# Expert weights loaded as one whole expert per block instead of half of two experts

## The reference

```
hg  = einsum('td,edf->tef', t, w_gate)     # 16 experts, 1024 -> 512
hu  = einsum('td,edf->tef', t, w_up)
act = silu(hg) * hu * combine              # two experts of one group per token
out = einsum('tef,efd->td', act, w_down)   # 512 -> 1024
```

## Time and profile before

| what | value |
| --- | --- |
| median of 3 runs | 2135.21 us (2132.83 to 2135.38) |
| the profiled execution's own time | 2134.79 us |
| its span, first to last instruction | 2133.0 us |
| TensorE matmul busy | 1902.6 us, 89% |
| TensorE weight load busy | 979.1 us, 46% |
| VectorE / ScalarE busy | 445.3 / 375.9 us |
| bytes moved by DMA | 597.12 MB, mean 280 GB/s |
| packets of SP's queue | 105840 of 583.29 MB |
| mean granted clock of TensorE | 0.935 of full speed |

### The profile page before, as it was taken

One profiled execution on the slowest core, in us unless ns is written; L12 is line 12 of the kernel. 1 busy time (PEld: TensorE's weight loads), 2 busy tenths in 40 slices (PEclk: granted clock), 3 DMA queues, 4 the chain that ended last, 5 costly groups with the idle time before them and its releaser, 6 DMA issues.

```text
span 2133.0 us, 19763 instructions
## 1 busy us (share of the span) xinstructions
PE 1902.6 (89%) x8458; PEld 979.1 (46%) x8458; DVE 445.3 (21%) x992; ACT 375.9 (18%) x674; POOL 67.2 (3%) x86
## 2 busy tenths in 40 slices
PE   3987899989998999989988899998999997899996
PEld 1552334436555334436544534335885654443432
DVE  0120011120053011120012201112345582201112
ACT  1120101111042101121010211002223341211111
POOL 1000000000000000000000000000002420000000
PEclk7988999999978999999999799999999999899998
DMA  9458999995842799985872299996341231379994
GB/s 341 190 225 354 421 418 420 421 368 212 342 176 79 320 411 421 420 339 197 316 276 79 79 413 421 419 421 258 120 161 55 80 104 49 119 291 420 416 422 205
DMA packets 109597, 597.12 MB, mean 280 GB/s; under 512 B 6208, under 2 KB 6304, under 8 KB 47936
## 3 DMA queue, kind: packets, MB, share of 16 engines
q1 hardware_dynamic: 105840, 583.29, 68.2%
q0 software_dynamic: 3664, 12.49, 1.8%
HBM read 591.56 MB, written 4.19 MB: 279 GB/s over the span
## 4 chain that ended last, share of the span: by engine, by line
PE 70%; DMA 20%; DVE 5%; ACT 4%; issue 1%; SPq 0%; POOL 0%; DVEq 0%; ACTq 0%; POOLq 0%
DMA ring<-in_moe_w_down 15%; PE psum L454 15%; PE psum L900 13%; PE psum L447 11%; PE psum L882 6%; PE psum L929 5%; PE psum L950 5%; DMA ring<-in_ada_w 4%; PE psum L480 3%; PE psum L513 2%; PE psum L851 1%; PE psum L795 1%; PE psum L778 1%; PE psum L779 1%; ACT arena L1271 1%
## 5 line engine op out<-in xcount | busy, mean ns | idle before, releaser
L900 PE MATMUL psum<-ring,arena 128*64 128x512 f32 x2048 | 449.6, 596 | 10.0 <-DMA ring<-in_moe_w_up 5.2
L900 PEld LDWEIGHTS psum<-ring,arena 128*64 128x64 f32 x2048 | 144.1, 137 | 300.7 <-issue 283.1
L929 PE MATMUL psum<-ring,arena 128*64 128x512 f32 x1024 | 234.5, 600 | 39.3 <-DMA ring<-in_moe_w_down 35.1
L447 PE MATMUL psum<-at,ring 128*128 128x256 f32 x1024 | 229.7, 387 | 4.5 <-ACT at L1075 4.5
L447 PEld LDWEIGHTS psum<-at,ring 128*128 128x128 f32 x1024 | 198.1, 194 | 38.5 <-ACT at L1075 5.6
L454 PE MATMUL psum<-ring,arena 128*128 128x512 f32 x384 | 169.9, 605 | 8.1 <-DVE arena L1533 5.7
L1673 DVE TENSOR_TENSOR arena<-arena,psum 128x512 f32<-128x512 f32 x32 | 33.7, 1053 | 656.8 <-PE psum L900 656.8
L929 PEld LDWEIGHTS psum<-ring,arena 128*64 128x64 f32 x1024 | 71.6, 137 | 195.6 <-issue 133.7
L454 PE MATMUL psum<-ring,at 128*128 128x512 f32 (+1 forms) x352 | 144.6, 565 | 0.0
L480 PE MATMUL psum<-ring,condT 128*32 128x512 f32 x768 | 104.8, 687 | 37.9 <-DMA ring<-in_ada_w 33.7
L882 PE MATMUL psum<-arena,xn 128*128 128x256 f32 x512 | 123.4, 403 | 8.7 <-DVE arena L1459 8.7
(11 more groups left out here) (240 smaller groups left out, 1400.0 us busy)
## 6 DMA issues: line engine op xcount, KB each, us to landing
ring<-in_moe_w_gate SPq DMA_DIRECT2D x64, 2048.0 KB, 13.8
ring<-in_moe_w_up SPq DMA_DIRECT2D x64, 2048.0 KB, 16.1
ring<-in_moe_w_down SPq DMA_DIRECT2D x64, 2048.0 KB, 10.8
ring<-in_ada_w SPq DMA_DIRECT2D x48, 2048.0 KB, 12.6
ring<-in_ssd_w_in SPq DMA_DIRECT2D x12, 2048.0 KB, 8.5
ring<-in_gmlp_w_in SPq DMA_DIRECT2D x8, 2048.0 KB, 11.4
ring<-in_na_w_qkv SPq DMA_DIRECT2D x6, 2048.0 KB, 15.5
ring<-in_gmlp_w_out SPq DMA_DIRECT2D x4, 2048.0 KB, 11.4
```

Of the source, the lines that this page charges most:

```text
L447: last = nc.tensor.matmul(dst, slot(k)[:, c, m * P:(m + 1) * P], src[:, c, :], start=(c == 0), stop=(c == nk - 1))
L900: last = nc.tensor.matmul(ps[b][e * CAP:(e + 1) * CAP, :], rows, slot_pair(k, 4)[:, e, c, :], start=(h == 0 and c == 0), stop=(h == 1 and ...
L929: last = nc.tensor.matmul(ps[6 + j][e * CAP:(e + 1) * CAP, :], actT[:, 2 * h + c, e * CAP:(e + 1) * CAP], slot_pair(k, 2)[:, e, c, j * SLO ...
```

## The change

An expert block now holds **all rows of one expert**: `G{x}.0` is the gate matrix of expert 2x and `G{x}.1` that of expert 2x + 1, and likewise for up and down. A partition's part of one block is then one contiguous run of 16 KB of the matrix instead of two runs of 8 KB. The number of blocks, their size, their order and the ring stay as they are.

Since the two experts of a pair are multiplied in alternation, row group by row group, a product now waits for both of its blocks before its first matmul, and frees both slots after its last one. The matmuls, their operands' shapes and their order are the same. The core of the diff:

```diff
-        def slot_pair(k, c):
+        def slot_expert(k, c):
-            return ring[:, k % RING, :].rearrange("p (e c n) -> p e c n", e=2, c=c)
+            return ring[:, k % RING, :].rearrange("p (c n) -> p c n", c=c)
...
-                    x, h = (int(v) for v in w[1:].split("."))
-                    c = 2 if w[0] == "D" else 4
+                    x, e = (int(v) for v in w[1:].split("."))
+                    c = FF // P if w[0] == "D" else DC
...
-                    load(k, slot_pair(k, c), rows[:, 2 * x:2 * x + 2, c * h:c * h + c, :])
+                    load(k, slot_expert(k, c), rows[:, 2 * x + e, :, :])
...
                 def pair_rows(x, w, b):
-                    for h in range(2):
-                        k = AT[n, f"{w}{x}.{h}"]
-                        arrive(k)
-                        for c in range(4):
-                            for e in range(2):
-                                rows = xg[:, x // 2 % 2, 4 * h + c, (x % 2) * P + e * CAP:(x % 2) * P + (e + 1) * CAP]
-                                last = nc.tensor.matmul(ps[b][e * CAP:(e + 1) * CAP, :], rows, slot_pair(k, 4)[:, e, c, :],
-                                                        start=(h == 0 and c == 0), stop=(h == 1 and c == 3))
-                        last.then_inc(slot_done, 1)
+                    k = AT[n, f"{w}{x}.0"]
+                    arrive(k)
+                    arrive(k + 1)
+                    for c in range(DC):
+                        for e in range(2):
+                            rows = xg[:, x // 2 % 2, c, (x % 2) * P + e * CAP:(x % 2) * P + (e + 1) * CAP]
+                            last = nc.tensor.matmul(ps[b][e * CAP:(e + 1) * CAP, :], rows, slot_expert(k + e, DC)[:, c, :],
+                                                    start=(c == 0), stop=(c == DC - 1))
+                    last.then_inc(slot_done, 2)
```

More of the change, by code:

```diff
@@ L922, in down_product @@
                     pe.wait_ge(y_ev, PAIRS * n + x)
[L923 to L932, removed]
+                    k = AT[n, f"D{x}.0"]
+                    arrive(k)
+                    arrive(k + 1)
+                    for c in range(FF // P):
+                        for j in range(2):
+                            for e in range(2):
+                                last = nc.tensor.matmul(ps[6 + j][e * CAP:(e + 1) * CAP, :], actT[:, c, e * CAP:(e + 1) * CAP],
+                                                        slot_expert(k + e, FF // P)[:, c, j * SLOT_COLS:(j + 1) * SLOT_COLS],
+                                                        start=(c == 0), stop=(c == FF // P - 1))
+                    last.then_inc(slot_done, 2)
                 def scatter(g):
```

## The result

The changed kernel takes **2349.53 us** (median of 4 runs, 2345.59 to 2351.08) against 2134.02 before: ratio 1.1008, 95% interval 1.0989 to 1.1027. It is slower, as forecast; 2342 was predicted, 7.5 us too little. The profiled execution has 2350.7 us and a span of 2348.9, 215.9 more than before.

A forecast was written before the change was run, and what follows sets the result against it. DMA was taken to set the expert stage's pace, TensorE close behind. Pair cycles 129.6, clock 48, starts 16, ends 16.4 and longer runs -3.4 add 206.6 us to 2134.8, about 2342 us with the median's 0.4; range 2276 to 2376.

The forecast's parts named there:

- the cycle that the prediction wrote down: Down product, transposes with gather or scatter, gate product, landing of two down blocks: 35.5 us instead of 30.1, before clock loss.
- 24 pair cycles with the clock's part and the gain of longer runs: Expert pairs in all layers: 129.6 us of longer cycles, plus 48 for the clock, minus 3.4 for longer runs.
- gain of longer runs: Expert weight DMA: 16 KB runs move 427 GB/s instead of 421, gaining 3.4 us on the path in all.
- starts of the four layers' experts: Pair 0's down blocks land later: 5.0 us in each of three layers, 1 us in layer 0, together 16.
- ends: Pair 6's second down landing to the end of a layer's experts: 4.1 us more in each of four layers, 16.4.
- mixers between: Between the layers' expert stages: no cost, since the next mixer's first four blocks have landed either way.
- ahead of the first expert product: Stretch before the expert products begin: no cost was counted, 0 us.
- Issue to landing of two blocks: Down blocks on an empty queue after the gate product: 8.1 us for the first, 5.0 for the second, 13.1 together.
- The clock: TensorE's clock falls in every wait before a down product, which then loses 2.0 us, 48 us over 24 cycles.
- Rival 1: The clock doesn't fall in the waits ahead of down products: 2284 us; chance 0.20, including a fall in only some waits.
- Waiting for both blocks in the up product's stage: Up product, between gate and down products: no waiting for its blocks was counted, 0 us.
- Rival 3: Expert stage: the DMA queue stays the bound and only its rate counts, 2122 us; chance 0.03.

The follow-up runs named there:

- 8 KB kernel: Kernel before with its old blocks in 8 KB runs, but each product waits for both blocks first and frees both slots at its end: 2354.36 us.
- kernel with the up product alone: Kernel before with whole-expert blocks, common wait and common release for the up product only, gate and down unchanged: 2178.46 us, ratio 1.0218.
- light kernel: Most expert matmuls left out, all blocks loaded, each waited for and freed singly: 2120.09 us with old blocks, 2108.05 us with whole-expert blocks and fewer matmuls.
- late-wait kernel: Kernel before with old blocks, both waited for ahead of a product's first matmul, each slot still freed after its half: 2231.95 us, ratio 1.0464.

## Why the prediction was right, step by step

The mechanism is shown: moving only the waits and releases gives the whole loss, the down product is where TensorE waits, and the loss falls in the cycle that the prediction wrote down. The measured cycle is 37.4 us (896.7 / 24 in the four layers) against 37.5. That agreement is partly luck: inside the cycle two terms are off by 0.4 us each, in opposite directions (below), some 9 us each over the 24 cycles.

| term | forecast | measured in the profile |
| --- | --- | --- |
| 24 pair cycles with the clock's part and the gain of longer runs | 129.6 + 48 - 3.4 = 174.2 | 896.7 - 723.3 = 173.4 |
| starts of the four layers' experts | 16 | 2.5 + 5.7 + 3.6 + 5.1 = 16.9 |
| ends | 16.4 | 4.77 + 4.07 + 4.88 + 4.98 = 18.7 |
| mixers between | 0 | -1.9 |
| ahead of the first expert product | 0 | 8.8 |
| sum | 206.6 | 215.9 |

(Starts run from the first gate product to pair 0's second down landing, ends from pair 6's down product to the next mixer's first matmul or the end.)

- **Issue to landing of two blocks**, forecast 13.1 us, and 13.0 with the gain of longer runs: measured 12.6 us on average over the 24 cycles (12.3 to 13.9). The 8 KB kernel's 13.27 us shows that 13.1 was nearly right for the runs from which its rows came. What was too small is the gain of longer runs: the forecast counted only the faster flow, 0.14 us per cycle, and the landing got 0.67 us shorter.
- **The clock**, forecast 2.0 us per wait: the 24 down products on the cycle take 9.48 us on average, where 7.1 is the undisturbed time, so 2.4 us. This took back what the shorter landing gave. (All down products' busy time rose by 59.5 us, from 234.5 to 294.0; but some half products before were slow already, as in the earlier trace rows, so the rise per wait, 2.1 us, is less.) Rival 1 priced the other world at 2284; with the waits in front of down products nearly filled, it is 2303.
- **Waiting for both blocks in the up product's stage**, costed at nothing. In layer 1's cycles of the changed kernel no wait stands between the gate and the up product; but the reason that I gave for a kernel with the up product alone was wrong (above).
- **The ahead-of-start term** is the main part of the difference between the two sums. Some 5 us of it stand before any changed block is used: the first gather (L882 in the kernel before) starts at 160.82 in this profile, at 155.52 before, and at 154.4 to 157.8 in the profiles of the twelve other kernels. So nothing ties it to the change; what delayed it is open. The other three executions of the changed kernel were about as long (2345.59 to 2351.08) and have no profile, so whether the median's 7.5 us come from there is not shown. The rest is the first gate product, which now waits for its second block.
- **Rival 3** (the queue stays the bound) needed a landing within 7.5 us; it was 12.6 on average. The rate behind its price was right: where the queue is kept full, 16 KB runs move 427 GB/s.

No version that beats the kernel before was found. The light kernel shows what there would be to gain, 421 to 427 GB/s, but with four slots of a whole block each, every tried way to use 16 KB runs gave back more.

## What to carry to other kernels

A ring's depth counts in units of what is waited for and freed together: with common waits and releases, four slots are two, and each product then closes a loop of its own (compute, release, latency, two landings). Write down that loop for every block that streams through the ring, with landing times taken from an empty queue, and compare it with the queue's own period before making transfers "better". Add the clock: here idle time of TensorE ahead of a long product cost more than itself. And compare term by term, not only the sum: in this case two misses cancelled inside a cycle that came out right.

## What the runs showed of the hardware

- Waits of 2 to 3.5 us within otherwise full work were mostly followed by a low clock, but not always: in the late-wait kernel, products behind waits of 2.99 and 3.43 us took 8.8 and 8.6 us instead of 7.1, and one behind 3.00 us took 7.09.
- Filling such a wait with matmuls that nobody reads kept the clock at 1.00 and took the changed kernel from 2349.53 to 2302.82 us.
- After the release that led to the issue of two 2 MB blocks, the product that waits for both started 13.27 us later with 8 KB runs and 12.60 us later with 16 KB runs (means of 24); with the queue never empty, the rate was 421 and 427 GB/s.
- 11 fp32 matmuls of 128x512 on the full array made 22 records and took 9.71 us, so 0.88 us each.
- Matmuls of two experts on different halves of the array's columns overlap even when the program has one wholly behind the other, but only around the change from one to the other (10 records in 2 us instead of 6; 41.3 us per pair against 50 expected).
